# Differential and sparse attention: query tiles from token 16 in falling order, and one tile of 16 meta tokens

## The chip, the cores and the metric

The kernel runs on one core of one Trainium2 chip. The metric is the device time of one execution in microseconds (us), from the first to the last instruction of the program and what lies around them. Three runs of the kernel before gave 2288.31, 2290.07 and 2291.01 us; their median, 2290.07 us, is the time before.

## The reference, cut to what matters

The program is a stack of six layers on 512 tokens of 1024 channels: a Mamba-2 mixer and a sliding-window attention first; then 16 learned meta tokens are put in front, which makes 528 tokens, and a differential attention, a feed-forward layer, a sparse attention and a second feed-forward layer follow. The change touches the two attentions over 528 tokens.

```python
# differential attention: 8 heads, two maps of 64 channels each, values of 128
s = jnp.einsum('bqhcd,bkhcd->bhcqk', qb, k)
s = jnp.where(k_pos[None, :] <= q_pos[:, None], s, -jnp.inf)     # causal
p = jax.nn.softmax(s, axis=-1)
a = p[:, :, 0] - lam * p[:, :, 1]
o = einsum('bhqk,bkhe->bqhe', a, v)
# sparse attention: 16 heads; an indexer scores the keys of each query
score = jnp.where(causal & (k_pos < N_META)[None, :], BIG_SCORE, score)
score = jnp.where(causal, score, -jnp.inf)
top_val, top_idx = lax.top_k(score, topk)        # topk = 128
p = softmax over those keys;  o = p @ v
```

Each token attends to itself and to earlier ones. In the sparse attention a token keeps the 16 meta keys and the best others, 128 in all, so a meta token sees plain causal attention among 16 keys. The result is the last 512 tokens after a final norm.

## The kernel before, in words

All five engines run programs written by hand, with semaphores between them; the order of the instructions in the source is the order on each engine. Activations lie transposed, channels on partitions and 528 tokens along the row. Every projection is three products of split float32 numbers (`product`, line 301): a high part of the weights is made by ACT (`high`, L260), a low part by DVE or POOL (`low_on_vector`, L276, `low`, L268), in slots that the weight stream of SP refills.

`pairs` is one stage of attention, called twice: with `diff` (prefix `da`, 8 heads) and without (prefix `dsa`, 8 pairs of heads of 64 channels). A turn of its loop does head (or pair) `s` and, beside it, the projections of head `s + 1`. Per head:

- ACT evicts the projections (L2004). With `diff`, ACT also issues four DMAs for the queries and four for the keys that swap their channels by 32 (L2011); without it, PE turns them by a product (`rot`, L1854). DVE makes the rotary sum (L2149 to L2158). PE transposes the values (L1862), ACT stores them (L2023, L2024); in the sparse stage ACT copies ready values (L2016, L2017).
- Five tiles of queries follow, `TILES[n]`: 128 queries from token 0, 128, 256 and 384, and 16 from token 512. For a tile that starts at token c with nq queries, keys 0 to c + nq are used. Per tile: scores on PE for two maps (`scores`, L1883) into one buffer S of PSUM, banks 2 to 5; DVE adds the mask and takes the maximum (L2171, L2174); ACT takes the exponential and the sum (`exps`, L2030); DVE divides (L2188 to L2198); PE transposes the result in blocks of 128 keys (`trans`, L1899); ACT copies the blocks (`store_pt`, L2038, L2040); PE multiplies them with the values (`pv`, L1912); ACT stores the output (`store_o`, L2045). `MAPS` is the order of the maps. With `diff` the two maps are joined before the transposes; without it each is transposed.

S is single: scores of tile n + 1 wait until both reductions of tile n are done. What PE does between them is written in `step` of the tensor program: projection pieces (24 matmuls, or two half pieces of 12) stand between tile n's scores and its transposes, and again before its `pv`. Tile 3's `pv` and tile 4's transposes and `pv` fall in the next turn. In the sparse stage the output lies in bank 3, columns 128 to 384, where tile 4's scores, 512 to 528, have their last 16 columns in the same bank; so `pv` of tile 3 waits for tile 4's reductions, and tile 4's scores for tile 2's output.

The last turn (`step(NI, lin=False)`) has no projections beside it, except that of the values in the differential stage.

`index` makes the sparse mask. Queries are taken from token 16 on in four chunks of 128; DVE takes eight maxima at a time and writes 0 or -1e30 into `kept` (L2451). `TILES` begins at token 0, so POOL moves `kept` by 16 partitions into `mb` with seven DMAs (`move`, L2269, L2270), and DVE waits for them at the sparse stage's first tile 1. DVE fills `mb` before (L2404 to L2406).

## Time and profile before

| | before |
|---|---|
| median of three runs | 2290.07 us |
| span of the profiled execution | 2287.3 us |
| PE busy | 2134.9 us (93%) |
| DVE busy | 1460.5 us (64%) |
| ACT busy | 1016.0 us (44%) |
| POOL busy | 47.9 us |
| differential loop, first scores of head 0 to those of head 7 | 789.18 to 999.40 us |
| sparse loop, the same | 1628.18 to 1817.02 us |

The profile names one execution. Its own time outside the span is not listed: the median lies 2.8 us above the span. PE is busy almost throughout, mostly with projections (L301). The two stages that are changed take 244 us (789 to 1033) and 217 us (1628 to 1845), two tenths of the time. In a row of a timeline the first number is the start in us from the beginning of the span, the second the duration, then engine, line, operation, output and inputs, shape and count; a bracket tells how long the engine stood idle before it, and what ended that. Matmul durations overlap a little, so differences of starts give the cost of one in a row of many.

### The profile page before, as it was taken

Reading aid. Unit: us, or ns where it says so; the run is one execution under the profiler, and the core shown is the slowest. Engines: PE = TensorE matmul, PEld = TensorE weight load, DVE = VectorE, ACT = ScalarE, POOL = GpSimd, SP = SyncE. Lnnn points to the kernel's source line nnn. Section 1 sums busy time; section 2 is a strip of 40 time slices with the busy share of each in tenths; the row PEclk is TensorE's granted clock in tenths of the full one; section 3 lists DMA queues with packets and bytes.
Section 4 is the critical chain, followed back from the end, with each engine's and each line's share of the span. In section 5 each row is a group of like instructions: output and inputs, shape, how many; then the busy total and the mean of one; then the engine's idle time right before and its main releaser. Section 6 shows DMA issues by size and latency. Waiting matters only on the chain. (4 is left out here: it accounts for less than half of the span.)

```text
span 2287.3 us, 39714 instructions
## 1 busy us (share of the span) xinstructions
PE 2134.9 (93%) x14439; PEld 1862.1 (81%) x14439; DVE 1460.5 (64%) x3050; ACT 1016.0 (44%) x1891; POOL 47.9 (2%) x37
## 2 busy tenths in 40 slices
PE   5999998889998799989999999999899889999998
PEld 3777786667766688869999999987777689999886
DVE  6677876547775777765566653369566656666532
ACT  3555563435553455653444432324455534444322
POOL 1000000000000000000000000122100000000000
PEclk8999998899999899979999999989999889999999
DMA  5533321252212222212323333401111122333331
GB/s 126 135 106 101 101 78 51 80 114 57 46 38 65 61 70 74 74 29 80 93 86 91 92 103 90 102 20 41 51 43 39 35 74 84 92 92 92 110 89 50
DMA packets 357001, 174.63 MB, mean 76 GB/s; under 512 B 60735, under 2 KB 352424, under 8 KB 356904
## 3 DMA queue, kind: packets, MB, share of 16 engines
q1 hardware_dynamic: 353192, 168.19, 26.9%
q10 hardware_dynamic: 3072, 4.33, 0.7%
q0 software_dynamic: 640, 0.87, 0.3%
q8 instruction: 55, 0.90, 0.2%
q14 instruction: 42, 0.34, 0.1%
HBM read 166.58 MB, written 2.16 MB: 74 GB/s over the span
## 5 line engine op out<-in xcount | busy, mean ns | idle before, releaser
L301 PE MATMUL ps<-h_parts,parts 128*128 128x264 f32 (+3 forms) x8576 | 1309.8, 311 | 31.0 <-DVE h_parts L670 12.0
L301 PEld LDWEIGHTS ps<-h_parts,parts 128*128 128x128 f32 x8576 | 1174.7, 191 | 124.7 <-issue 38.0
L260 ACT ACTIVATE parts<-ring 128x1024 fp32r<-128x1024 f32 (+1 forms) x282 | 307.3, 1092 | 687.6 <-PE ps L301 457.8
L276 DVE TENSOR_TENSOR parts<-ring,parts 128x1024 fp32r<-128x1024 f32 (+1 forms) x266 | 337.1, 1270 | 172.7 <-ACT parts L260 171.6
L301 PE MATMUL ps<-wide_parts,parts 128*128 128x264 f32 (+3 forms) x1040 | 323.4, 325 | 0.0
L301 PE MATMUL ps<-up_hidden,parts 128*128 128x264 f32 (+1 forms) x1056 | 241.4, 322 | 1.8 <-PEq L2512 1.8
L301 PEld LDWEIGHTS ps<-wide_parts,parts 128*128 128x128 f32 x1040 | 193.0, 191 | 16.3
L301 PEld LDWEIGHTS ps<-up_hidden,parts 128*128 128x128 f32 x1056 | 175.1, 188 | 17.4 <-issue 2.1
L2495 DVE TENSOR_TENSOR up_u<-ps,norm_rstd 128x264 f32<-128x264 f32 (+2 forms) x176 | 74.9, 427 | 160.5 <-PE ps L301 153.1
L2811 DVE TENSOR_TENSOR res<-ps,res 128x264 f32<-128x264 f32 (+3 forms) x56 | 25.9, 467 | 98.0 <-PE ps L301 91.6
L301 PE MATMUL ps<-gated_high,parts 128*128 128x512 f32 x256 | 82.5, 402 | 2.5 <-DVE wide_parts L1230 2.0
L1883 PE MATMUL ps<-wide 64*128 64x256 f32 (+5 forms) x384 | 75.4, 484 | 7.7 <-DVE wide L2158 6.7
L1899 PEld LDWEIGHTS ps<-cst,wide 128*128 128x128 f32 (+2 forms) x360 | 36.1, 146 | 52.5 <-issue 28.5
L1042 DVE SCALAR_TENSOR_TENSOR ssm_conv<-wide,vec,ssm_conv 128x512 f32<-128x512 f32 x96 | 71.9, 751 | 8.6 <-ACT ssm_dts L772 1.9
L2505 DVE SCALAR_TENSOR_TENSOR up_hidden_plain<-up_u,vec,up_hidden_plain 128x528 f32<-128x528 f32 (+1 forms) x88 | 66.9, 760 | 10.4 <-DVE up_hidden_plain L2503 4.0
L268 POOL TENSOR_TENSOR parts<-ring,parts 128x1024 fp32r<-128x1024 f32 x16 | 38.3, 2397 | 1562.8 <-ACT parts L260 1562.8
L2482 ACT ACTIVATE up_hidden_plain<-up_u,vec 128x528 f32<-128x528 f32 (+1 forms) x88 | 71.0, 807 | 0.0
L1899 PE MATMUL ps<-cst,wide 128*128 128x128 f32 (+2 forms) x360 | 52.5, 271 | 17.6 <-DVE wide L2198 9.0
L2171 DVE CUSTOM_DVE_ANT_0 wide<-ps,mb 128x128 f32<-128x128 f32 (+4 forms) x80 | 42.1, 526 | 37.9 <-PE ps L1883 35.4
L2503 DVE SCALAR_TENSOR_TENSOR up_hidden_plain<-up_u,vec,up_hidden_plain 128x528 f32<-128x528 f32 (+1 forms) x88 | 66.3, 753 | 0.0
L2030 ACT ACTIVATE wide<-wide,dsa_nm 128x128 f32<-128x128 f32 (+4 forms) x80 | 47.1, 591 | 37.2 <-DVE dsa_nm L2174 37.2
L301 PEld LDWEIGHTS ps<-gated_high,parts 128*128 128x128 f32 x256 | 49.0, 191 | 15.9 <-issue 3.5
(321 smaller groups left out, 2331.8 us busy)
## 6 DMA issues: line engine op xcount, KB each, us to landing
ring<-in_ffn_w_up SPq DMA_DIRECT2D x88, 512.0 KB, 3.8
ring<-in_ssm_w_in SPq DMA_DIRECT2D x48, 512.0 KB, 4.1
ring<-in_ffn_w_down SPq DMA_DIRECT2D x32, 704.0 KB, 4.6
ring<-in_da_w_qkv SPq DMA_DIRECT2D x24, 512.0 KB, 4.1
ring<-in_dsa_w_in SPq DMA_DIRECT2D x24, 512.0 KB, 3.8
ring<-in_att_w_in SPq DMA_DIRECT2D x40, 256.0 KB, 3.7
ssm_prefix<-prefix_rows SPq DMA_DIRECT2D x32, 256.0 KB, 4.1
ring<-in_ssm_w_out SPq DMA_DIRECT2D x16, 512.0 KB, 4.2
```

Of the source, the lines that this page charges most:

```text
L260: self.nc.scalar.activation(self.part(st, u, 0), self.slot(x, st.kt), ACT.Copy).then_inc(self.w_high, 1)
L276: self.nc.vector.tensor_tensor(self.part(st, u, 1), self.slot(u % st.ring, st.kt), self.part(st, u, 0).bitcast(F32), ALU.subtract).then_in ...
L301: m = self.nc.tensor.matmul(out, w[:, n], b, start=start and f == j == 0, stop=stop and f == st.kt - 1 and j == 2)
L1042: ins = v.scalar_tensor_tensor(acc, u[:, q, j:j + SEQ], k.col(V_CW + 32 * j + tile), acc, ALU.mult, ALU.add)
L1883: m = nc.tensor.matmul(S[0:nq, x, lo:hi], rop[h, 0, c:N], rop[h, 1, lo:hi], start=True, stop=True)
L1899: m = nc.tensor.transpose(TP[0:w, x, b * nq:(b + 1) * nq], pn[0:nq, x, a:a + w], k.ident[0:nq, 0:nq])
L2030: nc.scalar.activation(p[0:nq, x, 0:c + nq], p[0:nq, x, 0:c + nq], ACT.Exp, bias=nm[0:nq, x:x + 1], scale=0.125, accum_out=den[0:nq, x:x + ...
L2171: v.tensor_tensor_reduce(p[0:nq, x, 0:N], S[0:nq, x, 0:N], mask(n), 1.0, -3e38, ALU.add, ALU.max, accum_out=mx[0:nq, x:x + 1]).then_inc(se ...
L2482: nc.scalar.activation(cc[:, x, begin:T2], u[:, x, begin:T2], ACT.Identity, scale=k.col(w0 + t), bias=k.col(w2 + 2 * FT + t)).then_inc(s_t ...
L2495: v.tensor_tensor(u[:, x, 2 + c:2 + c + w], ps[:, 2 + (2 * x + b) % 4, 0:w], k.rstd[:, c:c + w], ALU.mult).then_inc(s_free, 1)
L2503: v.scalar_tensor_tensor(acc, u[:, x, 1 + begin:1 + T2], k.col(w0 + 2 * FT + t), acc, ALU.mult, ALU.add).then_inc(s_mid, 1)
L2505: v.scalar_tensor_tensor(acc, u[:, x, 2 + begin:2 + T2], k.col(w2 + t), acc, ALU.mult, ALU.add).then_inc(s_conv, 1)
```

## The change

A second table of tiles, `QUERIES`, serves the queries: 128 from token 400, 272, 144 and 16, in this order, then 16 from token 0. Keys and values stay in blocks that start at multiples of 128 (`blocks`), so a tile of queries that starts at 16 + 128 m ends with a block of 16 keys. The mask of the indexer has the same four tiles and is written in place into `mb`, in the order of use; the moves on POOL, their semaphore and the buffer `kept` go. For the first chunk the causal mask is added on DVE, since a query with fewer than 112 keys behind the meta tokens would keep later ones too. The meta tile takes its mask from `maskb`. The last block of tile 0's transposes, 16 rows by 128 columns per map, goes to bank 5 (`TPL`), and its copy `ptl` is 128 wide. Tile 4's scores are 16 wide and stay clear of bank 3, so the wait for tile 2's output before them and the wait for their reductions before tile 3's `pv` go. ACT increments a semaphore once more per head (`passed`).

```diff
--- before.py
+++ after.py
@@ -43,6 +43,7 @@
 TILES = [(a, min(P, T2 - a)) for a in range(0, T2, P)]
+QUERIES = [(META + a, P) for a in range(SEQ - P, -1, -P)] + [(0, META)]
 LAMBDA_INIT = 0.2
@@ -169,7 +170,6 @@
         self.granted = self.sem("refills_granted")
-        self.mask_moved = self.sem("mask_moved")
         self.passed = self.sem("waits_passed")
@@ -1788,7 +1788,7 @@
         pt, mx, nm, den, rd = sb("pt", [P, maps, 512]), sb("mx", [P, 2]), sb("nm", [P, 2]), sb("den", [P, 2]), sb("rd", [P, 2])
-        ptl = sb("ptl", [META, maps, META])
+        ptl = sb("ptl", [META, maps, P])
         osq, lnv, rstd = (k.wide[:, j, :] for j in range(19, 22)) if diff else (None,) * 3
@@ -1806,13 +1806,18 @@
         def mask(n):
-            c, nq = TILES[n]
-            return sheet[0:nq, SEQ - c:SEQ + nq] if diff else mb[0:nq, n, 0:c + nq]
+            c, nq = QUERIES[n]
+            if diff:
+                return sheet[0:nq, SEQ - c:SEQ + nq]
+            return mb[:, n, 0:c + nq] if c else k.maskb[0:nq, P:P + nq]
         O = ps[:, 7, :] if diff else ps[:, 3, P:3 * P]
 
+        TPL = ps[0:META, 5, P:3 * P].rearrange("p (x j) -> p x j", x=2)
+
         def blocks(n):
 
-            return [(b, *TILES[b]) for b in range(n + 1)]
+            c, nq = QUERIES[n]
+            return [(b, b * P, min(P, c + nq - b * P)) for b in range((c + nq + P - 1) // P)]
 
@@ -1823,13 +1828,9 @@
                 if not diff:
-                    first, move = pool_first
-                    first(pool)
-                    for m in range(1, 4):
-                        move(pool, m)
+                    pool_first(pool)
                     for at in ((0, 0), (0, 1), (1, 0)):
                         k.low(pool, st, at)
-                    move(pool, 4)
 
@@ -1863,7 +1864,7 @@
                 def scores(s, n):
-                    c, nq = TILES[n]
+                    c, nq = QUERIES[n]
                     N = c + nq
@@ -1871,8 +1872,6 @@
                         pe.wait_ge(sem["masked"], 10 * s + 2 * n)
-                        if n == 4 and not diff:
-                            pe.wait_ge(sem["o"], 5 * s + 3)
                         if n == 4:
@@ -1884,7 +1883,7 @@
                 def trans(s, n):
-                    _, nq = TILES[n]
+                    _, nq = QUERIES[n]
                     if n == 0:
@@ -1896,20 +1895,19 @@
                         for b, a, w in blocks(n):
-                            m = nc.tensor.transpose(TP[0:w, x, b * nq:(b + 1) * nq], pn[0:nq, x, a:a + w], k.ident[0:nq, 0:nq])
+                            to = TP[0:w, x, b * P:b * P + nq] if b < 4 else TPL[:, x, :]
+                            m = nc.tensor.transpose(to, pn[0:nq, x, a:a + w], k.ident[0:nq, 0:nq])
                     m.then_inc(sem["t"], 1)
...
                 def pv(s, n):
-                    _, nq = TILES[n]
+                    _, nq = QUERIES[n]
                     pe.wait_ge(sem["pt"], 5 * s + n + 1)
                     wait(pe, sem["o"], 5 * s + n)
-                    if n == 3 and not diff:
-                        pe.wait_ge(sem["masked"], 10 * s + 10)
                     for b, a, w in blocks(n):
...
                             d = slice(0, P) if diff else slice(64 * x, 64 * x + 64)
-                            r = pt[0:w, x, b * nq:(b + 1) * nq] if b < 4 else ptl[:, x, :]
-                            m = nc.tensor.matmul(O[d, 0:nq], vt[0:w, b, d], r, start=b == 0, stop=b == n)
+                            r = pt[0:w, x, b * P:b * P + nq] if b < 4 else ptl[:, x, :]
+                            m = nc.tensor.matmul(O[d, 0:nq], vt[0:w, b, d], r, start=b == 0, stop=w < P)
                     m.then_inc(sem["pv"], 1)
@@ -2024,23 +2022,22 @@
                 def exps(s, n):
-                    c, nq = TILES[n]
+                    c, nq = QUERIES[n]
                     for j, x in enumerate(MAPS):
...
                 def store_pt(s, n):
-                    _, nq = TILES[n]
                     act.wait_ge(sem["t"], 5 * s + n + 1)
                     wait(act, sem["pv"], 5 * s + n)
-                    if n == 4:
-                        nc.scalar.activation(ptl[:], TP[0:META, 0:maps, 4 * META:5 * META], ACT.Copy)
-                    w = min(n + 1, 4) * nq
-                    nc.scalar.activation(pt[:, :, 0:w], TP[:, 0:maps, 0:w], ACT.Copy).then_inc(sem["pt"], 1)
+                    if n == 0:
+                        nc.scalar.activation(ptl[:], TPL[:, 0:maps, :], ACT.Copy)
+                    w, rows = (min(5 - n, 4) * P, P) if n < 4 else (META, META)
+                    nc.scalar.activation(pt[0:rows, :, 0:w], TP[0:rows, 0:maps, 0:w], ACT.Copy).then_inc(sem["pt"], 1)
 
                 def store_o(s, n):
-                    c, nq = TILES[n]
+                    c, nq = QUERIES[n]
                     act.wait_ge(sem["pv"], 5 * s + n + 1)
@@ -2068,6 +2065,7 @@
                     act.wait_ge(sem["o"], 5 * s + 5)
+                    act.sem_inc(k.passed, 1)
                     nc.scalar.activation(osq, head(s), ACT.Square).then_inc(sem["osq"], 1)
@@ -2159,13 +2157,11 @@
                         k.low_on_vector(dve, st, st.after(s, 1, st.depth))
-                    for n, (c, nq) in enumerate(TILES):
+                    for n, (c, nq) in enumerate(QUERIES):
                         N = c + nq
...
                         dve.sem_inc(k.passed, 1)
-                        if not diff and n == 1 and isinstance(s, int) and s == 0:
-                            dve.wait_ge(k.mask_moved, 16 * 7)
                         for j, x in enumerate(MAPS):
@@ -2235,12 +2231,11 @@
     wiT, wi = k.wide[:, 16, :], sb("wi", [P, 5, NH])
-    kept = sb("kept", [P, CHUNKS, SEQ], BF16)
     kn, lnv, rstd = (k.wide[:, j, :] for j in (12, 13, 14))
...
         "lin_done", "lin_free", "wi_product", "squares", "summed", "rstd", "kn", "rot", "rope", "scores", "relu", "acc", "m"))
-    s_kept, s_moved = k.sem("idx_kept"), k.mask_moved
+    s_kept = k.sem("idx_kept")
     s_rtok = k.sem("idx_rstd_by_token")
@@ -2260,14 +2255,6 @@
         k.low_all(pool, vst)
-
-    def move(pool, m):
-
-        pool.wait_ge(s_kept, m)
-        if m > 1:
-            w = min(P * m, SEQ) - META
-            pool.dma_start(mb[META:P, m - 1, META:META + w], kept[0:P - META, m - 1, 0:w]).then_inc(s_moved, 16)
-        pool.dma_start(mb[0:META, m, META:META + P * m], kept[P - META:P, m - 1, 0:P * m]).then_inc(s_moved, 16)
 
@@ -2401,9 +2388,7 @@
         pre.dve(dve)
-        do(v.memset(mb[:], NEG))
-        do(v.memset(mb[:, 1:5, 0:META], 0.0))
-        do(v.tensor_copy(mb[:, 0, 0:P], k.maskb[:, P:2 * P]))
+        do(v.memset(mb[:, :, 0:META], 0.0))
         pre.rstd_ready(dve)
@@ -2448,10 +2433,15 @@
                 do(v.match_replace(row, m8[:], row, -3e38))
-            v.tensor_scalar(kept[:, n - 1, 0:N], row, -2e38, NEG, ALU.is_gt, ALU.mult).then_inc(s_kept, 1)
+            own = mb[:, CHUNKS - n, META:META + N]
+            if n == 1:
+                do(v.tensor_scalar(own, row, -2e38, NEG, ALU.is_gt, ALU.mult))
+                v.tensor_tensor(own, own, k.maskb[:, P:2 * P], ALU.add).then_inc(s_kept, 1)
+            else:
+                v.tensor_scalar(own, row, -2e38, NEG, ALU.is_gt, ALU.mult).then_inc(s_kept, 1)
             dve.wait_ge(s_kept, n)
         steps.end()
-    return sync_program, (pool_program, move), pe_program, act_program, dve_program
+    return sync_program, pool_program, pe_program, act_program, dve_program
 
@@ -2845,7 +2835,7 @@
         with ExitStack() as own:
-            mb = k.sb("mb", [P, 5, T2], BF16, own)
+            mb = k.sb("mb", [P, CHUNKS, T2], BF16, own)
             vall = k.sb("values", [P, 8, 5, P], F32, own)
```

PE's program in the differential loop, from the first scores of a head on. L1883 (now L1882) are the scores, L1862 (L1863) the value transposes, L301 a projection, L1919 (L1917) the squares of the head before. Before:

```order
L1883 MATMUL ps<-wide 128x128 x2
L1858 REGISTER_ALU
L91 REGISTER_ALU
L1862 MATMUL ps<-cst,wide 128x128 x4
L1862 MATMUL ps<-cst,wide 16x128
L279 ISA
L91 ISA
L301 MATMUL ps<-h_parts,parts 128x264 x24
L1919 MATMUL ps<-wide,cst 128x264 x2
```

Now:

```order
L1882 MATMUL ps<-wide 128x512 x2
L1882 MATMUL ps<-wide 128x16 x2
L1859 REGISTER_ALU
L92 REGISTER_ALU
L1863 MATMUL ps<-cst,wide 128x128 x4
L1863 MATMUL ps<-cst,wide 16x128
L279 ISA
L92 ISA
L301 MATMUL ps<-h_parts,parts 128x264 x24
L1917 MATMUL ps<-wide,cst 128x264 x2
```

The head's widest scores stand first; everything around them keeps its place.

The end of the same loop, from tile 2's `pv` (L1912, now L1910) to tile 3's transposes (L1899). Before:

```order
L1912 MATMUL ps<-da_pt,da_v 128x128 x3
L1873 REGISTER_ALU
L1883 MATMUL ps<-wide 16x512 x2
L1883 MATMUL ps<-wide 16x16 x2
L1894 REGISTER_ALU
L1899 MATMUL ps<-cst,wide 128x128 x4
```

Now:

```order
L1910 MATMUL ps<-da_pt,da_v 128x128 x3
L1874 REGISTER_ALU
L1882 MATMUL ps<-wide 16x16 x2
L1893 REGISTER_ALU
L1899 MATMUL ps<-cst,wide 128x128
L1899 MATMUL ps<-cst,wide 16x128
```

Tile 4's scores shrink from 528 to 16 columns, and tile 3 has two blocks instead of four.

The sparse loop, from the first scores to the first transposes. Before:

```order
L1883 MATMUL ps<-wide 128x128 x2
L301 MATMUL ps<-h_parts,parts 128x264 x12
L1873 REGISTER_ALU
L1883 MATMUL ps<-wide 128x256 x2
L1894 REGISTER_ALU
L1899 MATMUL ps<-cst,wide 128x128 x2
```

Now:

```order
L1882 MATMUL ps<-wide 128x512 x2
L1882 MATMUL ps<-wide 128x16 x2
L301 MATMUL ps<-h_parts,parts 128x264 x12
L1874 REGISTER_ALU
L1882 MATMUL ps<-wide 128x400 x2
L1893 REGISTER_ALU
L1899 MATMUL ps<-cst,wide 128x128 x4
L1899 MATMUL ps<-cst,wide 16x128
L1899 MATMUL ps<-cst,wide 128x128 x4
L1899 MATMUL ps<-cst,wide 16x128
```

Between tile 0's and tile 1's scores stands half a projection, as before; the transposes are ten instead of two.

## Rows read from the trace of the kernel before

**Rows 1.** Windows, core 0: busy time and instructions of each engine, granted clock, DMA.

```profile
820.00:999.00 179.00, 172.73 (x1326) 150.78 (x1324) 129.95 (x387) 104.27 (x290) 0.00 (x0) 1.00 0.24 68
1655.00:1800.00 145.00, 138.79 (x1175) 110.86 (x1174) 99.48 (x326) 77.24 (x215) 0.00 (x0) 1.00 0.18 47
1006.00:1034.00 28.00, 17.92 (x64) 10.66 (x64) 17.80 (x51) 15.05 (x39) 0.00 (x0) 0.56 0.00 1
```

**Rows 2.** Timeline of PE, one turn: start, duration, line, shape, idle and releaser.

```profile
849.87 0.49 PE L1883 MATMUL ps<-wide 64*128 64x128 f32 x4
...
855.67 0.32 PE L1899 MATMUL ps<-cst,wide 128*128 128x128 f32 x1
...
863.67 1.13 PE L1883 MATMUL ps<-wide 64*128 64x512 f32 x4
...
868.26 0.83 PE L1912 MATMUL ps<-da_pt,da_v 128*128 128x128 f32 x6
...
870.02 0.66 PE L1899 MATMUL ps<-cst,wide 128*128 128x128 f32 x4
...
873.44 1.06 PE L1912 MATMUL ps<-da_pt,da_v 128*128 128x128 f32 x8
...
875.13 0.41 PE L1899 MATMUL ps<-cst,wide 16*128 16x16 f32 x5 [0.64 <-DVE wide L2198]
...
879.74 0.49 PE L1883 MATMUL ps<-wide 64*128 64x128 f32 x4
```

**Rows 3.** Timeline of ACT, its DMA queue and DVE, the same turn.

```profile
852.47 0.39 ACT L2030 ACTIVATE wide<-wide,da_nm 128x128 f32<-128x128 f32 x1
...
853.95 0.35 DVE L2198 SCALAR_TENSOR_TENSOR wide<-wide,da_rd 128x128 f32<-128x128 f32 x1
...
868.88 2.44 ACTq L2011 DMA_DIRECT2D da_turned<-wide  x4
...
871.62 0.59 ACT L2040 ACTIVATE da_pt<-ps 128x512 f32<-128x512 f32 x1
...
872.10 0.72 ACT L2030 ACTIVATE wide<-wide,da_nm 16x528 f32<-16x528 f32 x1
...
874.23 0.76 DVE L2198 SCALAR_TENSOR_TENSOR wide<-wide,da_rd 16x528 f32<-16x528 f32 x1
...
878.59 0.71 DVE L2158 TENSOR_TENSOR wide<-wide 128x528 f32<-128x528 f32 x1
```

**Rows 4.** Timeline of PE, one turn of the sparse loop.

```profile
1708.12 0.49 PE L1883 MATMUL ps<-wide 64*128 64x128 f32 x4 [0.16 <-DVE wide L2158]
...
1710.19 0.70 PE L1883 MATMUL ps<-wide 64*128 64x256 f32 x4
...
1711.33 0.44 PE L1899 MATMUL ps<-cst,wide 128*128 128x128 f32 x2 [0.44 <-DVE wide L2192]
...
1724.05 1.08 PE L1883 MATMUL ps<-wide 64*16 64x512 f32 x8
...
1734.94 0.49 PE L1883 MATMUL ps<-wide 64*128 64x128 f32 x4 [0.15 <-DVE wide L2158]
```

**Rows 5.** Timeline of DVE, tile 4 of the same sparse turn.

```profile
1725.37 0.70 DVE L2171 CUSTOM_DVE_ANT_0 wide<-ps,mb 16x528 f32<-16x528 f32 x1 [3.08 <-PE ps L1883]
...
1728.12 0.48 DVE L2192 TENSOR_SCALAR wide<-wide,dsa_rd 16x528 f32<-16x528 f32 x1
```

**Rows 6.** Timeline of PE, last heads: differential first, then sparse.

```profile
999.40 0.49 PE L1883 MATMUL ps<-wide 64*128 64x128 f32 x4
...
1028.62 2.10 PE L1919 MATMUL ps<-wide,cst 128*128 128x264 f32 x4 [1.04 <-ACT wide L2071]
...
1806.84 1.78 PE L1912 MATMUL ps<-dsa_pt,dsa_v 128*64 128x128 f32 x16 [1.89 <-DVE dsa_mx L2171]
...
1817.02 0.80 PE L1883 MATMUL ps<-wide 64*128 64x128 f32 x4 [1.61 <-DVE wide L2158]
```

**Rows 7.** Timeline of DVE, between index stage and sparse loop.

```profile
1615.97 0.71 DVE L2149 TENSOR_TENSOR wide<-wide,rcos 128x528 f32<-128x528 f32 x1 [5.96 <-ACT wide L2004]
```

## The prediction, made before the changed kernel was run

> **What bounds the kernel now.** I read the page first: TensorE (PE) is the busiest engine and ends the program, so its waits are the first suspects. Then the windows over the two attention loops [rows 1]: in the differential loop PE is busy 172.73 of 179 us, in the sparse loop 138.79 of 145 us, both at granted clock 1.00; when a stage has no projection left beside its last head, PE falls to 17.92 of 28 us and the clock to 0.56, the lower level of 1.2 GHz. Then the timeline of one turn on every engine, since a loop's period can be closed by a chain that PE's busy share hides.
>
> Differential turn: from one first score product to the next are 879.74 - 849.87 = 29.87 us [rows 2]. Only one wait shows there, 0.64 us before the last tile's transposes, ended by DVE's division (L2198). The rows of ACT and DVE show what lies behind it [rows 3]. ACT issues four DMAs (L2011), 2.44 us, in which nothing else starts on it; only then come the copy of the transposes (871.62), the exponentials of tile 4 (872.10), DVE's division (874.23) and its rotary chain for the next head, done 878.59 + 0.71 = 879.30. The next first scores start at 879.74: this chain is 0.3 us from setting the period already.
>
> Sparse turn: 1734.94 - 1708.12 = 26.82 us, with small waits, the largest shown 0.44 us before the first transposes [rows 4].
>
> **The change, part by part: widths.** Before, a head's five tiles are 128, 256, 384, 512 and 528 keys wide (the last with 16 queries); after, 528, 400, 272, 144 and 16. 1808 columns become 1360. The blocks of 128 keys or less stay 15, but their order turns from 1, 2, 3, 4, 5 to 5, 4, 3, 2, 1. Prices at full clock [rows 2]: scores 0.49 us for 128 columns and 1.13 for 512, so 0.0017 us a column; a block of pV 1.06 - 0.83 = 0.23; a block of transposes (0.66 - 0.32) / 3 = 0.11 per map. The 16 extra keys of the new first tile need small matmuls with a 128-column load; no row shows them. The bounds are nothing and the 0.49 us of the 128-column product; I take 0.25.
>
> **Differential loop.** I cut the turn where pV of tile 2 starts (868.26), since ACT's issue stall follows there. The part before it is 868.26 - 849.87 = 18.39 us. Its scores get 64 more columns and the small matmuls, +0.35; pV of tiles 0 and 1 has 9 blocks instead of 3, +1.38; transposes of tiles 0 to 2 have 12 instead of 6, +0.66; about 0.4 of small gaps around the 512-column products and the first transposes goes (as walked product by product). 20.3 us, give or take 0.2. Does a wait appear in it? The widest tile is now first: value copies (L2023, L2024) on ACT hold its exponentials back, now to 852.47 - 849.87 = 2.6 us after the scores began, with 0.9 us longer scores to 3.5. From the exponential to the division's end the 528-wide tile takes 874.23 + 0.76 - 872.10 = 2.89 us, so transposes can go at 6.6. PE is there at 855.67 - 849.87 = 5.8 now (the transposes of tile 0 stand behind the value transposes, a projection, the squares and tile 1's scores), and with the longer scores at 6.8. No wait, by 0.2 us.
>
> The part after it is 11.48 us now, of which 0.64 is the wait. PE alone would need 10.84 less 0.9 (scores of 16 instead of 528 columns), 0.2 (two transposed blocks less), 0.45 (two pV blocks less), and 1.25 (the last tile has one block instead of five): 8.0 us. But the chain is: ACT reaches the copy of the transposes 871.62 - 868.26 = 3.36 us after the cut, whatever the tile; that copy is 256 instead of 512 wide, some 0.26 instead of 0.48 to the next instruction; from the exponential to the division's end it takes 2.89 us at 528 columns and 853.95 + 0.35 - 852.47 = 1.83 at 128, so 1.53 at 16 on that line. The division ends at 5.15. Then DVE's cosine products and four more rotary instructions, which are not changed, 878.59 + 0.71 - 874.99 = 4.31, and 0.15 for the semaphore. Sum 9.6. 20.3 + 9.6 = 29.9 against 29.87: **nothing gained in a loop in which PE loses work and most of a 0.64 us wait**. What PE saves becomes a wait of 0.9 us before the first scores, with some 0.6 left before the last transposes. The cover that hides the saving is this chain; if it had slack, the turn would be 20.3 + 8.0 = 28.3. If the 16-wide tile costs what 128 columns do, the turn is 0.3 longer. Seven turns: 0, between -11 and +2.
>
> Here a rule of the Trainium skill speaks against the change. The page VectorE: DVE Perf Modes, section on the TRN2 errata, says that an SBUF-source instruction of VectorE or ScalarE pays a fixed latency whatever its width, and advises tiles of at least 512 elements. The trace agrees in kind: 0.35 us at 128 columns against 0.76 at 528 [rows 3]. By the page's table, 224 + 16 cycles at 1.2 GHz, the small exponential would be estimated at 0.20 us; the sum would move by under 1 us in all.
>
> **Differential, last head.** No projection stands beside it, and its path is a chain of round trips, 1028.62 - 999.40 = 29.2 us [rows 6]. It loses 448 columns, each worth 0.0033 us of scores at the low clock (twice 0.0017), 0.001 of reduction, 0.0017 for two exponentials (0.72 us at 528), 0.001 of division: 0.007, so -3.1 us at most. Widths are partly hidden by spread copies and low parts between; I take -3.0, since the very narrow last round trips have nothing beside them; bounds -5 and 0.
>
> **Sparse loop.** One S buffer serves all tiles: tile 1's scores wait for tile 0's reductions. Scores of 528 columns end at 1.45 us; the first reduction starts 0.24 later (as 1725.37 does after the product that ends at 1725.13), at 1.69; both are done 1.6 on, so scores of tile 1 start at 3.33, and PE with only half a projection between (1710.19 - 1708.12 = 2.07 now, less 0.42 for the first product: 1.65) is ready at 3.03: a wait of 0.3. From the first reduction to the last division is 1728.12 + 0.48 - 1725.37 = 3.23 [rows 5]; the transposes can go at 4.98, PE is ready at 4.20: a wait of 0.8. These two replace the 0.44 and a smaller one. From first scores to the last tile's scores (15.93 us now [rows 4]): +0.35 scores, pV 12 blocks instead of 6 +1.32, transposes 14 instead of 10 on two maps +0.84, waits +0.4: 18.8. From there to the next head (10.89 now): scores of 16 instead of 528 -0.86, pV of two blocks instead of four -0.44, transposes 2 instead of 10 -0.49, last pV 4 instructions instead of 20 -0.6: 8.5. Turn 27.3, +0.5, six times +3.0. If both new waits (1.1 together) were hidden, the six turns would come to -3.5; if both doubled, to +9.5.
>
> **Last turn and last head of the sparse stage** [rows 6]. The seventh turn has the longer front (+2.4), and behind it no projection: there PE waits 1.89 us for the reduction because pV's output shares a bank with the 512:528 columns. That wait goes, and the narrow tile's chain shortens: 12.1 us from the last scores' end to 1817.02 become 9.3. Together -0.4. The last head by the same walk -0.4, because its blocks, of two maps, cost as much as they did at 1.2 GHz; at most -3 by the columns.
>
> **Index stage.** Two memsets and a copy shrink to one memset, the seven moves leave POOL's DMA queue (and the projection splits queued behind them on it no longer wait), the mask is written in place, one 128-column addition is added. DVE has 5.96 us idle after that stage, waiting for ACT's evictions [rows 7]: 0. What would be late if that cover were gone is the first rotary product. The extra semaphore increment on ACT: 0.
>
> **Sum**: 0 - 3.0 + 3.0 - 0.4 - 0.4 = -0.8 us on a span of 2287.3 us, which lies 2.8 us under the median of the runs, 2290.07. Forecast 2289.3 us, no change: this kernel's measurement tells no less than 0.2%, 4.6 us.
>
> **Rivals.**
> 1. *Faster: PE bounds the differential loop.* For it: PE 172.73 of 179 us busy there. Against: the chain over ACT's issues and DVE's rotary products. Turn 28.3, or 28.9 with the wait before the last transposes left: -11 to -7 us, time 2278 to 2282. A sparse loop whose two new waits are hidden gives -6.5, alone 2283. Together 0.26.
> 2. *Slower: the differential tail does not shrink.* The part before the cut grows 1.9 us for certain; the part after it shrinks only if a 16-wide tile's exponential, reduction and division are really short. For it: fixed latency. Against: 0.35 against 0.76 us. If they stayed as at 528 columns, only the copy would be shorter and the turn 1.4 longer: +10 us, 2299. It decides from 0.8 us a turn. 0.12.
> 3. *Slower: the sparse waits are double*: +6.5 us, 2296. For it: reduction, exponential and division of the widest tile stand there with half a projection beside them. Against: no part of their chain is unmeasured [rows 5]. 0.07. A granted clock that falls in these gaps would end here too; the differential loop keeps 1.00 with its 0.64 us wait.
> The forecast: 0.55. Its own range is 2285 to 2294. The 80% range reaches to the faster rivals and the near end of the slower: 2280 to 2297. Faster 0.26, same 0.55, slower 0.19.
>
> **What would show it.** Differential turn 29.9 us, PE waiting about 0.9 us for DVE's rotary sum (L2156 now) before 512-column scores: if that wait is missing and the turn is under 29, rival 1. Turn over 30.7: rival 2. Sparse turn 27.3 with waits of 0.3 (before scores of 400) and 0.8 (before the first transposes). No 1.89 us wait before the last pV products. Both last heads end earlier by 3.0 and 0.4. Most likely to be wrong: the 0.2 us margin at the first transposes, and the cold last heads, walked from hot prices.

## The result, and the profile after

| | before | changed |
|---|---|---|
| median of 20 runs each | 2288.89 us | 2293.10 us |
| ratio of the two, 95% interval | | 1.0021 [1.0012, 1.003] |
| span of the profiled execution | 2287.3 us | 2292.6 us |
| PE busy | 2134.9 us | 2138.0 us |
| DVE busy | 1460.5 us | 1440.5 us |
| differential stage, first scores to first output product (da_out) | 244.90 us | 246.84 us |
| sparse stage, the same (dsa_out) | 217.05 us | 221.23 us |
| differential turn, in the loop | 29.85 us | 30.39 us |
| sparse turn, in the loop | 26.82 us | 27.66 us |

By the ratio the changed kernel is 0.21% slower, about 4.8 us of 2289 (the two medians differ by 4.2), and the interval lies clear of 1. Forecast was no change, 2289.3 us. The median of after lies inside the range that was given, but there is a loss where none was forecast: the terms that had to cancel did not.

Windows after: the first two over the same stretches as [rows 1], the third inside the last differential head, where no projection stands (columns as there: PE, PEld, DVE, ACT, POOL busy, granted clock, DMA share, GB/s):

```profile
820.00:999.00 179.00, 173.36 (x1317) 152.77 (x1317) 117.69 (x383) 101.34 (x289) 0.00 (x0) 1.00 0.25 68
1655.00:1800.00 145.00, 136.31 (x1130) 109.37 (x1129) 91.23 (x306) 72.45 (x200) 0.00 (x0) 1.00 0.16 44
1014.00:1030.00 16.00, 11.09 (x42) 6.97 (x42) 10.32 (x40) 8.70 (x27) 0.00 (x0) 0.50 0.00 1
```

Over these stretches DVE has 12 us less work in the differential loop and 8 less in the sparse loop, as the narrower tiles promise; it bought nothing. Windows over exactly one turn tell more. First one differential and one sparse turn of before, then the same of after:

```profile
879.74:909.59 29.85, 28.90 (x223) 25.24 (x222) 22.18 (x65) 17.91 (x50) 0.00 (x0) 1.00 0.25 71
1708.12:1734.94 26.82, 25.59 (x219) 20.50 (x219) 18.22 (x58) 14.27 (x39) 0.00 (x0) 1.00 0.15 39
```

```profile
882.06:912.46 30.40, 29.21 (x223) 25.77 (x223) 20.73 (x65) 17.50 (x51) 0.00 (x0) 1.00 0.24 70
1710.98:1738.64 27.66, 26.13 (x218) 21.06 (x218) 17.08 (x58) 14.13 (x39) 0.00 (x0) 1.00 0.14 38
```

The columns of scores of a head fell by a quarter (1808 to 1360), and PE's busy time rose: by 0.3 us a differential turn and by 0.54 a sparse one. The rest of each turn's growth (0.24 and 0.30) is waiting.

The end of a differential turn after, which answers to [rows 2, 3]: timelines of PE, of ACT with its queue, and of DVE (start, duration, line, idle time ahead and what ended it).

```profile
872.16 1.02 PE L1910 MATMUL ps<-da_pt,da_v 128*128 128x128 f32 x6
...
876.43 0.80 PE L1910 MATMUL ps<-da_pt,da_v 128*128 128x128 f32 x4
877.44 0.17 PE L1899 MATMUL ps<-cst,wide 16*16 16x16 f32 x1 [0.21 <-DVE wide L2194]
...
882.06 0.70 PE L1882 MATMUL ps<-wide 64*128 64x512 f32 x2 [0.98 <-DVE wide L2156]
```

```profile
872.78 2.44 ACTq L2009 DMA_DIRECT2D da_turned<-wide  x4
875.35 0.28 ACT L2042 ACTIVATE wide<-ps 128x128 f32 x1 [1.66 <-issue]
875.53 0.38 ACT L2037 ACTIVATE da_pt<-ps 128x256 f32<-128x256 f32 x1
875.79 0.29 ACT L2028 ACTIVATE wide<-wide,da_nm 16x16 f32<-16x16 f32 x1
```

```profile
877.07 0.22 DVE L2194 SCALAR_TENSOR_TENSOR wide<-wide,da_rd 16x16 f32<-16x16 f32 x1
877.61 1.33 DVE L2147 TENSOR_TENSOR wide<-wide,da_rcos 128x528 f32<-128x528 f32 x2 [0.31 <-issue]
...
881.30 0.71 DVE L2156 TENSOR_TENSOR wide<-wide 128x528 f32<-128x528 f32 x1
```

Read upward from the last row of each: the scores wait 0.98 us for DVE's rotary sum (881.30 + 0.71). That rotary chain starts behind tile 4's division. The division waits for an exponential, and the exponential stands behind 2.44 us of DMA issue. One link is no work at all: for 0.31 us DVE stands between two instructions with no releaser but "issue".

The sparse turn after, PE alone, which answers to [rows 4]:

```profile
1710.98 1.26 PE L1882 MATMUL ps<-wide 64*128 64x512 f32 x8 [0.15 <-DVE wide L2156]
...
1714.06 0.94 PE L1882 MATMUL ps<-wide 64*128 64x400 f32 x4 [0.17 <-DVE dsa_mx L2167]
1715.84 1.31 PE L1899 MATMUL ps<-cst,wide 128*128 128x128 f32 x10 [0.84 <-DVE wide L2188]
...
1718.55 1.09 PE L1910 MATMUL ps<-dsa_pt,dsa_v 128*64 128x128 f32 x16
1719.57 0.43 PE L1910 MATMUL ps<-dsa_ptl,dsa_v 16*64 16x128 f32 x4
...
1723.07 1.24 PE L1910 MATMUL ps<-dsa_pt,dsa_v 128*64 128x128 f32 x16
...
1726.95 1.02 PE L1910 MATMUL ps<-dsa_pt,dsa_v 128*64 128x128 f32 x12
...
1733.26 0.80 PE L1910 MATMUL ps<-dsa_pt,dsa_v 128*64 128x128 f32 x8
```

Against them the rows of pV before, in the turn of [rows 4], for tiles of one, two, three and four full blocks:

```profile
1713.20 0.44 PE L1912 MATMUL ps<-dsa_pt,dsa_v 128*64 128x128 f32 x4
...
1716.46 0.66 PE L1912 MATMUL ps<-dsa_pt,dsa_v 128*64 128x128 f32 x8
...
1720.71 0.88 PE L1912 MATMUL ps<-dsa_pt,dsa_v 128*64 128x128 f32 x12
...
1728.17 1.09 PE L1912 MATMUL ps<-dsa_pt,dsa_v 128*64 128x128 f32 x16
```

The two waits are those that were forecast. The pV rows hold what was not: four full blocks take 1.09 us, and three full blocks with one of 16 keys behind them take 1.24; so 1.02 against 0.88 and 0.80 against 0.66.

The stage times also hold a disturbance that comes in some executions only. In the first differential turn after (788.94 to 821.64, 32.70 us against 30.16 before), four DMAs took 3.70 us to issue instead of 2.44; PE waited 0.61 and 0.51 us, and then the granted clock fell for four microseconds. Windows of after:

```profile
816.00:818.00 2.00, 1.49 (x9) 1.41 (x9) 1.93 (x5) 0.45 (x2) 0.00 (x0) 0.74 0.41 129
818.00:820.00 2.00, 2.00 (x11) 2.00 (x11) 1.90 (x4) 0.00 (x0) 0.00 (x0) 0.50 0.00 0
820.00:822.00 2.00, 2.00 (x14) 1.77 (x15) 0.61 (x1) 0.57 (x2) 0.00 (x0) 0.90 0.00 0
```

A projection of 24 products that takes 3.18 us elsewhere took 4.71 there. Four more profiled executions below have the same code in this turn. In e1 and e7 the issue took 2.45 us, no such wait came, and the turn took 30.47 and 30.52. In e9 and e11 the issue took 3.96 and 3.76 us, the waits and the fall of the clock came again, and the turn took 32.97 and 32.85. The two executions with the old code of this stage that issue from ACT (before, e2) had 30.16 and 30.19. What lengthens the issue is not known, nor is it shown that the old code never meets it. A stage's total of one execution carries some 2.4 us of this; the turns inside the loops repeat to 0.03 us, and the experiments are read by them.

### The profile page after: what moved, and what is told of

It reads as the page before. It is cut to its first block and busy times, and to the rows that moved or that the text cites. A ratio compares the mean times of both kernels' runs of the same rounds, so it can differ in the third digit from the quotient of the medians.

```text
span 2292.6 us, 39704 instructions
## 1 busy us (share of the span) xinstructions
PE 2138.0 (93%) x14439; PEld 1867.5 (81%) x14439; DVE 1440.5 (63%) x3049; ACT 1012.3 (44%) x1891; POOL 44.6 (2%) x30
## 3 DMA queue, kind: packets, MB, share of 16 engines
q1 hardware_dynamic: 353192, 168.19, 26.8%
## 5 line engine op out<-in xcount | busy, mean ns | idle before, releaser
L301 PE MATMUL ps<-h_parts,parts 128*128 128x264 f32 (+3 forms) x8576 | 1310.2, 311 | 31.0 <-DVE h_parts L670 11.9
L301 PEld LDWEIGHTS ps<-h_parts,parts 128*128 128x128 f32 x8576 | 1174.9, 191 | 126.1 <-issue 38.8
L276 DVE TENSOR_TENSOR parts<-ring,parts 128x1024 fp32r<-128x1024 f32 (+1 forms) x266 | 337.1, 1270 | 172.0 <-ACT parts L260 170.9
L301 PE MATMUL ps<-wide_parts,parts 128*128 128x264 f32 (+3 forms) x1040 | 324.1, 326 | 0.0
L301 PE MATMUL ps<-up_hidden,parts 128*128 128x264 f32 (+1 forms) x1056 | 241.4, 322 | 1.7 <-ACTq L2502 0.9
L301 PEld LDWEIGHTS ps<-wide_parts,parts 128*128 128x128 f32 x1040 | 193.6, 192 | 16.3
L301 PEld LDWEIGHTS ps<-up_hidden,parts 128*128 128x128 f32 x1056 | 175.1, 188 | 17.4 <-issue 2.1
L301 PE MATMUL ps<-gated_high,parts 128*128 128x512 f32 x256 | 82.4, 402 | 2.6 <-DVE wide_parts L1230 2.0
L1882 PE MATMUL ps<-wide 64*128 64x16 f32 (+5 forms) x384 | 62.6, 416 | 14.3 <-DVE wide L2156 11.4
L1899 PE MATMUL ps<-cst,wide 128*128 128x128 f32 x360 | 57.3, 290 | 11.8 <-DVE wide L2188 7.3
L1899 PEld LDWEIGHTS ps<-cst,wide 128*128 128x128 f32 x360 | 36.0, 130 | 35.6 <-issue 18.0
L2167 DVE CUSTOM_DVE_ANT_0 wide<-ps,da_causal 128x528 f32<-128x528 f32 (+4 forms) x80 | 34.7, 434 | 44.7 <-PE ps L1882 44.1
L301 PEld LDWEIGHTS ps<-gated_high,parts 128*128 128x128 f32 x256 | 49.0, 191 | 16.0 <-issue 3.5
L2002 ACT ACTIVATE wide<-ps 128x264 f32<-128x264 f32 x80 | 30.7, 385 | 67.2 <-PE ps L301 65.2
```

The costliest lines, as they stand in the source:

```text
L276: self.nc.vector.tensor_tensor(self.part(st, u, 1), self.slot(u % st.ring, st.kt), self.part(st, u, 0).bitcast(F32), ALU.subtract).then_in ...
L301: m = self.nc.tensor.matmul(out, w[:, n], b, start=start and f == j == 0, stop=stop and f == st.kt - 1 and j == 2)
L1882: m = nc.tensor.matmul(S[0:nq, x, lo:hi], rop[h, 0, c:N], rop[h, 1, lo:hi], start=True, stop=True)
L1899: m = nc.tensor.transpose(to, pn[0:nq, x, a:a + w], k.ident[0:nq, 0:nq])
L2167: v.tensor_tensor_reduce(p[0:nq, x, 0:N], S[0:nq, x, 0:N], mask(n), 1.0, -3e38, ALU.add, ALU.max, accum_out=mx[0:nq, x:x + 1]).then_inc(se ...
```

## Experiments

Theory A, formed on these traces: a differential turn is closed by a chain through ACT, DVE and PE, not by PE's work; the differential tail holds ACT's DMA issue in it, and the sparse turn pays for PE's work on 16-key blocks and for waits behind the widest tile. Rivals: the loss sits in one stage only, or in other stages; PE's own work closes the loops; or order alone is the cause. All medians are set against runs of before on the same chip.

### One stage at a time (e1, e2)

```diff
-            pairs(k, "da", S["da"], following["da"], True, update, spread=heads)
+            pairs_da(k, "da", S["da"], following["da"], True, update, spread=heads)
...
# e1: the kernel before, pairs_da being pairs of the changed one
# e2: the changed kernel, pairs_da being pairs of the kernel before
```

> The differential stage alone takes the new query tiles; the index and the sparse stage stay as before. Theory A (each stage loses on its own: the loops are closed by a chain over ScalarE, VectorE and the first scores, not by TensorE): this kernel is about 1.7 us slower than before (first da_out product +1.7 us: turns 210.2 to 214.3 us, last head -2.1), the wait of TensorE ahead of the first scores 0.98 us in a steady turn of 30.39. Rival B (the whole loss is in the sparse stage, and the differential shift is the clock of that one execution): within 0.5 us of before. Rival C (the tables in SBUF and the longer program cost the other stages too): more than 3 us slower.

> The index and the sparse stage alone take the new tiles; the differential stage stays as before. Theory A: +4.2 us in the sparse stage (first sparse scores to first dsa_out product 217.05 to 221.2 us; steady turn 26.8 to 27.66), whole time 3 to 4 us over before. Rival B: all of it, +4.8 us. Rival C (only the first turns and the ends differ, and steady turns are the same within 0.2 us when on the same chip): under 1.5 us slower.

Measured: e1 1.0004 [0.9993, 1.0015], median 2288.33; e2 1.0019 [1.001, 1.0028], median 2291.97. Turns in e1: differential 30.39, sparse 26.8; in e2: 29.87 and 27.66. So a stage's turn does not care what the other stage does. **The loss that the whole time shows is the sparse stage's**, 4.3 us (2.3 to 6.4). The differential stage is worth +0.9 us, -1.6 to +3.4: not told from nothing. In the traces its turns cost more (first scores of head 0 to head 7: 212.13 us in e1, 210.22 before, 210.00 in e2), and its last head gives it back (30.82 us to the first da_out product, 34.68 before and in e2). Its first turn in e1 was one of the undisturbed ones. Rival B, which put all of it in the sparse stage, is as good a reading of the times as A.

### The DMA issue out of the chain (e3, e4)

```diff
             def _(pool):
+                if diff:
+                    for i in range(NI):
+                        for u in range(2):
+                            pool.wait_ge(sem["lin_free"], NP * i + 2 * u + 2)
+                            wait(pool, sem["rope"], 2 * i - 1 + u if i else 0)
+                            for r in range(0, P, 32):
+                                pool.dma_start(turned[r ^ 32:(r ^ 32) + 32, u, :], raw[r:r + 32, u, :]).then_inc(s_turned[u], 16)
...
-                                if diff and j < 4:
-                                    turn(i, j // 2)
```

> The changed kernel with the eight DMAs a head that fill the turned copy of the query and key tiles in the differential stage issued by the idle GpSimd engine, and not by ScalarE (nothing is left out). Theory A (the differential turn is closed by ScalarE's 2.44 us of DMA issue, then the last tile's copy, exp and division, then the rotary chain): the last tile's exp starts about 2.4 us earlier, the 0.98 us wait ahead of the first scores goes, and TensorE bounds the turn at 28.9 to 29.4 us: 6 to 9 us faster than the changed kernel. Rival D (TensorE's own work and its other waits close the loop): the turn stays at 30.4 within 0.3 us. Rival E (GpSimd's issue is slow, so that the turned copy of the key arrives late): the turn is longer, the second rotary product waits for the DMA, 2 us or more slower.

> The kernel before with the same DMAs issued by GpSimd in the differential stage (nothing is left out). Theory A: before, the issue lay beside TensorE's work, whose wait ahead of the first scores was short, so a turn gains at most 0.6 us: 2 to 5 us faster than before over seven turns, clearly less than the same edit gives the changed kernel. Rival D: the turn stays at 29.85 within 0.3 us. Rival E: slower by 2 us or more, as in the changed kernel.

Measured: e3 0.9985 [0.9977, 0.9994], against 1.0021 without the edit; e4 0.9988 [0.9979, 0.9997]. Turns: e3 29.45 in the loop, from 30.39, and 29.0 to 29.1 outside it, but for the first, 31.12, which began at a granted clock of 0.50 that held some 6.5 us; e4 29.63, from 29.85. One turn of e3, then two rows of its DMA issue on GpSimd:

```profile
879.83:909.28 29.45, 29.04 (x222) 25.72 (x222) 20.64 (x65) 17.34 (x50) 3.93 (x8) 1.00 0.26 72
```

```profile
861.34 1.96 POOL L1836 DMA_DIRECT2D da_turned<-wide  x4 [16.71 <-ACT wide L2009]
871.74 1.96 POOL L1836 DMA_DIRECT2D da_turned<-wide  x4 [8.44 <-ACT wide L2009]
```

PE's 29.04 us of work is now nearly the whole turn, but 0.41 us of waiting for DVE's rotary sum are left, so that the turn lies just over the 28.9 to 29.4 expected. The exponential starts 1.86 us after tile 2's pV instead of 3.63 (in e3 from 870.86), and the division ends at 4.20 instead of 5.13: 2.44 us of issue bought 0.93. DVE's split of the weights (L276, 1.23 us, 872.84 to 874.07) now stands where the exponential stood, and the reciprocal for the division starts behind it, at 873.98. Theory A held: the same edit is worth 0.94 us a turn to the changed kernel and 0.22 to the kernel before. In e3 rivals D and E fell. In e4 E fell, but 0.22 lies within the 0.3 that D allowed, and only the whole time (2.7 us, 0.7 to 4.8) speaks against D there.

### The same engine, another place (e10)

```diff
+                            if diff and lin and q == 5:
+                                turn(i, 1)      # behind exps(s, 4), no longer in pieces()
```

> The changed kernel with ScalarE still issuing the DMAs of the turned tiles in the differential stage, but those of the key tiles (four in each head from the second) behind the last tile's exp and not ahead of its copy; nothing is left out. Theory A (it is the place of the 2.44 us issue in the closing chain that costs, not which engine does it): the last tile's exp starts about 2.4 us earlier, and the turn falls from 30.39 to 29.3 to 29.7 as long as the turned key tile still lands before VectorE's second rotary product. Rival F (the DMA lands too late now): VectorE waits for it, the wait ahead of the first scores grows over 0.98, turn 30.4 to 31.5. Rival D (the issue was never in the chain): turn unchanged at 30.39.

Measured: turn 30.24 us, whole time 1.0018 [1.0007, 1.0029]. The exponential starts 1.85 us after tile 2's pV (897.96) instead of 3.63, 1.8 us earlier and not 2.4, and the division ends 0.93 earlier, as in e3. But DVE's chain now stops for the DMA; its timeline in e10:

```profile
902.47 1.33 DVE L2149 TENSOR_TENSOR wide<-wide,da_rcos 128x528 f32<-128x528 f32 x2 [0.31 <-issue]
903.94 0.71 DVE L2154 TENSOR_TENSOR wide<-da_turned,da_rsin 128x528 f32<-128x528 f32 x1
904.68 0.71 DVE L2158 TENSOR_TENSOR wide<-wide 128x528 f32<-128x528 f32 x1
906.21 0.71 DVE L2154 TENSOR_TENSOR wide<-da_turned,da_rsin 128x528 f32<-128x528 f32 x1 [0.81 <-DMA da_turned<-wide]
```

Less that 0.81 us the turn would be 29.43, which is e3's 29.45. My 29.3 to 29.7 missed because of this landing: 906.21 lies 3.7 us after the last issue ended (902.52). That is rival F's mechanism: PE's wait ahead of the first scores grew from 0.98 to 1.19 us, though the turn stayed below F's 30.4. The chain is confirmed, and moving its stall inside ScalarE only trades it.

### DVE's loop written out (e7)

```diff
-                with dve.Fori(2, NI - 2) as s:
-                    step(s)
+                for s in range(2, NI - 2):      # the differential stage alone
+                    step(s)
```

> The changed kernel with VectorE's four looped turns of the differential stage written out one after another (nothing is left out). Theory: the 0.31 us that VectorE idles for its loop's branch, between the last division and the cosine products, stands in the closing chain now, so that the differential turn goes from 30.39 to 29.95 us in the turns that were looped, and the wait ahead of the first scores from 0.98 to 0.55; 1.2 to 1.8 us in all, too little for the whole time to tell. Rival: the gap is hidden, as it was before, and the turn stays at 30.39.

Measured: the three turns of 30.39 take 29.90; the wait ahead of the scores is 0.49. Whole time 1.001 [0.9998, 1.0021], not told apart from either kernel. The cosine products begin right behind the division (875.59, the division from 875.44 on for 0.22 us), and from the division's end to the end of the rotary sum pass 4.22 us instead of 4.72. So the gap of 0.31 us and what goes with it at the end of DVE's loop stood in the chain. Before, at the same place, the cosine products began at 874.91, right behind the 528-wide division of [rows 3]: there the gap did not show.

### Start and order apart (e5, e6)

```diff
-QUERIES = [(META + a, P) for a in range(SEQ - P, -1, -P)] + [(0, META)]
+QUERIES = [(META + a, P) for a in range(0, SEQ, P)] + [(0, META)]            # e5
...
+ORDER = [3, 2, 1, 0, 4]                         # e6: before, TILES[ORDER[n]] for TILES[n]
```

> The changed kernel with its query tiles still beginning at token 16, but in rising order (144, 272, 400, 528 keys, then the meta tile), in both stages; nothing is left out. The sparse stage needs two waits moved with it, since the 528-key scores now come beside an output. Theory W (in the sparse turn of 27.66 us the loss of 0.84 is 0.54 of TensorE's own work for the four 16-key blocks, which stays, and 0.30 of waits, which the falling order adds): sparse turn 27.2 to 27.4, the waits of 0.84 and 0.17 us replaced by short ones ahead of the first transposes. Rival O (the order is all of it): sparse turn 26.8. In the differential stage the theory of the closing chain says that the front is short again and the tail is that of a 16-key tile: the turn becomes 29.0 to 29.6, bound by TensorE; a rival says that the tail closes the loop whatever stands ahead of it: 30.4.

> The kernel before with its query tiles still beginning at token 0 but the four tiles of 128 in falling order (512, 384, 256, 128 keys), then the 16 queries with 528 keys as before; nothing is left out. Theory W: no 16-key blocks, so TensorE's work is that of before (25.6 us in the sparse turn), and the falling order costs its 0.3 us of waits: sparse turn 27.0 to 27.2. Rival O (the order is all of it): 27.6. Rival P (the blocks are all of it): 26.8. Differential stage: the front is long and the tail is the long one of 528 keys: the turn becomes longer than either kernel's, 31.0 to 32.0 us.

Measured: e5 1.0032 [1.002, 1.0045]; e6 1.0059 [1.0047, 1.0072]. The sparse turn falls apart into work and waits:

| sparse turn, us | turn | PE busy | the rest |
|---|---|---|---|
| start 0, rising (before) | 26.82 | 25.59 | 1.23 |
| start 16, falling (changed) | 27.66 | 26.13 | 1.53 |
| start 16, rising (e5) | 27.67 | 26.15 | 1.52 |
| start 0, falling (e6) | 27.39 | 25.69 | 1.70 |

The work follows the start, 0.44 to 0.56 us by pair, whatever the order: that half of theory W is shown. My numbers for the turns were 0.3 too low in both, because the waits are not a property of the order alone. In e5 the 528-key scores have to wait for an output in the same bank, which cost 0.56 us ahead of them; in e6 the falling order costs 0.47 and not 0.3. Rivals O and P fell: neither order nor blocks are all of it.

In the differential stage e6 gave two values. Three turns took 30.35, where 31 to 32 was expected: PE's idle went to one wait of 1.64 us ahead of the last transposes, and the chain behind it ran beside the last projection. Three others took 32.50 (the first), 31.83 and 31.90, and this is not the chain but the granted clock. Two turns of e6 from that wait on:

```profile
939.84 0.41 PE L1900 MATMUL ps<-cst,wide 16*128 16x16 f32 x5 [1.64 <-DVE wide L2201]
940.18 3.18 PE L302 MATMUL ps<-h_parts,parts 128*128 128x264 f32 x24
...
970.19 0.41 PE L1900 MATMUL ps<-cst,wide 16*128 16x16 f32 x5 [1.64 <-DVE wide L2201]
970.53 4.73 PE L302 MATMUL ps<-h_parts,parts 128*128 128x264 f32 x24
```

The wait is the same, and so is the work ahead of it; the clock stayed at 1.00 in the first and fell to 0.50 for some 3.5 us in the second, which made the projection 1.55 us longer. All seven turns of e6 have this wait (1.58 to 1.64), and it was followed by the fall in three. So two turns fell into the expected range, but for a reason that was not given. e5 missed: it gave 30.41 and not 29.0 to 29.6. Its waits in one turn (line waited for, us, times, longest):

```profile
PE ps L1863 <- ACT wide L2046: 0.6, 1, 0.6
PE ps L1901 <- DVE wide L2198: 0.3, 1, 0.3
```

The first is the value transposes standing for the last head's output copy. With the scores no longer late, the next wait in the ring appears at once, and at full clock all four orders lie at 29.85 to 30.43 in the loop.

### The short blocks left out (e9)

```diff
-            return [(b, b * P, min(P, c + nq - b * P)) for b in range((c + nq + P - 1) // P)]
+            return [... if diff or not c or b * P < c + nq - META]   # sparse: no last 16 keys
```

> The changed kernel, but in the sparse stage the four tiles of 128 queries leave out the last 16 keys of each: neither their transposes nor their products with the values are made (part of the computation is left out, and the output differs). Theory: a block of 16 keys costs TensorE what a full one does, 0.22 us of transposes and 0.36 to 0.43 us of products, four times a turn: TensorE's busy time in the sparse turn falls from 26.13 to about 23.7 us and the turn from 27.66 to 25.4 to 25.9, about 13 us over the stage. Rival 1 (the blocks are small and cheap): busy time falls by under 1 us. Rival 2 (VectorE and ScalarE close the sparse turn): busy time falls but waits take its place, and the turn stays over 27.0.

Measured, with the values of 16 keys missing in every such tile: sparse turn 25.58 us, PE busy 23.94, whole time 0.9933 [0.9916, 0.9949]. One turn of e9:

```profile
1708.49:1734.08 25.59, 23.94 (x195) 19.60 (x195) 17.04 (x58) 14.10 (x39) 0.00 (x0) 1.00 0.15 41
```

Work fell by 2.19 us and the turn by 2.08, so in the sparse turn PE's work counts nearly one for one, and sixteen keys cost 2.19 / 4 = 0.55 us a tile. Both rivals fell.

### The projection beside the widest tile (e11)

```diff
-        slots = [parts[0:2]] + [parts[j:j + 1] for j in range(2, 8)]
+        slots = [parts[0:1], parts[1:2], parts[2:4]] + [parts[j:j + 1] for j in range(4, 8)]
```

> The changed kernel with one half projection of the sparse stage moved: two half projections stand between the scores of the widest tile and those of the next, and one instead of two beside the meta tile (nothing is left out). Theory: the waits of 0.17 us before the 400-column scores and 0.84 before the first transposes come from having only half a projection beside the widest tile's reduction, exponential and division; with 1.65 us more work there both go. Beside the meta tile the division ends 0.1 us after TensorE could use it, and the rotary chain ends about 1.6 us earlier, so that 0.1 to 0.3 us of wait comes back: sparse turn 26.8 to 27.0 instead of 27.66, 4 to 5 us in all. Rival (what goes at the front comes back at the tail, because VectorE's chain closes the turn): 27.5 to 27.7.

Measured: 0.9974 [0.9963, 0.9985], sparse turn 26.77 us. Timeline of PE in e11, front and end of a turn:

```profile
1710.67 3.18 PE L301 MATMUL ps<-h_parts,parts 128*128 128x264 f32 x24
1713.78 0.94 PE L1882 MATMUL ps<-wide 64*128 64x400 f32 x4
1714.66 1.31 PE L1899 MATMUL ps<-cst,wide 128*128 128x128 f32 x10
...
1733.48 1.16 PE L1855 MATMUL ps<-wide,cst 128*128 128x264 f32 x4 [0.37 <-ACT wide L2042]
```

Both waits at the front are gone and nothing of them came back at the tail. The turn is 0.89 shorter at the same work (26.15 busy). Six such turns are 5.3 us, and the sparse stages of the two traces differ by 4.9 (221.23 and 216.37). The whole time fell by more: from 1.0021 to 0.9974, with 6.2 us between the near ends of the intervals. The two ratios come from different chips, and the profiled execution of e11 was the longest of its eight (2290.40 against a median of 2284.62), so its stages are not those of the median. What lies beyond the turns is left open.

### Put together (e8, e12)

e8 is e1 with the edits of e3 and e7 (new tiles in the differential stage alone); e12 is the changed kernel with those of e3, e7 and e11.

> A version meant to beat both: the new tiles in the differential stage alone, its DMAs for the turned tiles issued by the idle GpSimd engine, VectorE's loop of that stage written out, and the index and sparse stages of before. Theory A: every differential turn 29.0 us (TensorE's work, no wait), first scores to the first da_out product about 237.5 us against 244.9 before, the sparse stage as before at 217 us: 2280 to 2284 us, 5 to 8 us faster than before, and 2 to 4 faster than the kernel before with the same DMAs moved. Rival: without the order's cost in the sparse stage nothing else changes and the first head and the last give back what the turns gain: 2286.

> The changed kernel, new tiles in both stages, with three things moved: the turned tiles' DMAs on GpSimd, VectorE's differential loop written out, and the half projection of the sparse stage beside the widest tile (nothing is left out). Theory: differential turn 29.0 us, sparse turn 26.8 to 27.0: 2276 to 2279 us, the same within 0.1% as the version with the sparse stage of before (2276.8). Rival: sparse turn 27.66 still, 2281 to 2283.

Measured: e8 0.9955 [0.9938, 0.9971], median 2276.84; e12 0.9954 [0.9938, 0.9969], median 2277.73. Both beat both kernels. Windows over one differential turn and one sparse turn of e12:

```profile
878.50:907.54 29.04, 29.04 (x224) 25.73 (x223) 20.39 (x65) 17.35 (x50) 3.93 (x8) 1.00 0.26 73
1698.03:1724.80 26.77, 26.14 (x219) 21.11 (x219) 17.09 (x58) 14.35 (x39) 0.00 (x0) 1.00 0.14 39
```

The differential turn has no wait left: PE busy 29.04 of 29.04. There the new order is 0.6 us a turn better than the old one with the same DMAs moved (e4, 29.63; its turn outside DVE's loop took 29.62, so that the branch has no part in this). But little of it is work saved on PE. Without its wait of 0.38 us ahead of the last transposes, e4's turn would be 29.25, as the kernel before without its 0.64 would be 29.23. So the new order saves PE some 0.2 us a turn from start to start, and nothing by its busy time (28.99 in e4); the rest is a wait that is gone. The median of e8 is 3 us under the near end of what was expected; its stages were 235.00 and 213.96 us, 2.5 and 3 shorter than I had them. For the sparse stage, whose code is that of before, this is again the place at which the clock fell: its seventh turn took 25.81 us, with the clock at 1.00 to its end.

## Why the prediction was wrong

**The differential turn.** Forecast 29.9, measured 30.39. The closing chain was right part for part, from one cut to the next: front 20.49 (20.3), ACT at the copy 3.37 after the cut (3.36), division ended 5.13 after it (5.15), PE waiting 0.98 us for DVE's sum (0.9), 0.21 left before the last transposes (0.6). The 0.2 us margin at the first transposes, named as most likely to be wrong, held. What was missing in the chain is 0.41 between the division's end and the end of the rotary sum: 882.01 - 877.29 = 4.72 instead of 4.31. In e7, without the loop, the same stretch is 4.22. I took the rotary rows of before as a fixed price, though they stood behind a wide instruction that hid the gap. Term "seven turns: 0": +1.9 in e1, +4.1 in the profiled execution with its disturbed first turn.

The other side of this term failed too, though the chain hid it: "PE alone" was reckoned at 20.3 + 8.0 = 28.3 us, 0.9 below the 29.23 of before. e8, in which nothing but PE bounds the turn, shows 20.53 + 8.49 = 29.02. Of the 0.5 us missing behind the cut, 0.19 is pV of the 272-key tile, whose block of 16 keys was priced as a full one, 0.14 stands in the starts of the two projections, and most of the rest in the last tile. There was next to no gain for the chain to hide.

**The differential last head.** Forecast -3.0; -2.1 in after, -3.9 in e1. Right, as far as the clock lets it be read: the two differ in when the granted clock fell (0.89 in the first 11 us of it after, 1.00 in e1), and before it was at 0.60 there.

**The sparse turn: the step that failed.** Forecast 27.3, measured 27.66, +5.6 us over six turns instead of +3.0. The waits were right: 0.17 and 0.84 for 0.3 and 0.8, and +0.30 in all for the +0.4 that I summed. Wrong was "pV 12 blocks instead of 6 +1.32 ... pV of two blocks instead of four -0.44". I priced every block at the 0.22 us of a full one. The four 128-query tiles take 1.45 (its two rows overlap by 0.07) + 1.24 + 1.02 + 0.80 = 4.51 us of pV, and took 0.44 + 0.66 + 0.88 + 1.09 = 3.07: +1.44 where I had +0.88. Each of the four blocks of 16 keys costs 0.36 us, 0.14 more than a full one. These 0.56 us, less 0.14 of scores and 0.1 of waits that were cheaper than I had them, are the missing 0.36 within 0.04. For the small matmuls in the scores I had given bounds, for those in pV none: the one form that no row showed was taken for a known one.

**Seventh turn and last sparse head.** Forecast -0.4 and -0.4, read as -2.11 and +0.67. Of the first, most is not the edit: the code of before took 28.64 us in its own trace, with the clock at 0.50 from the 1.89 us wait on, and 25.78 in e1, where the clock fell some 6 us later; the changed code took 25.73 in e2. By these two the edit is worth nothing there. The old code also took 28.63 (e4) and 25.81 (e8), the changed code 26.51 to 26.70 in e3, e7 and e10, so that the term stays open within the clock's 2.9 us. The last head (28.21 before, 28.88 after, 26.55 in e2) moves more with the clock than with the edit; its term stays open.

**Index stage.** Forecast 0. From the first da_out product to the first sparse scores: 594.10 us before and 592.29 after, but 596.27 in e1 with the old code and 594.30 in e2 with the new. Over all traces it lies between 593.69 and 598.40 with the old code and between 592.27 and 598.44 with the new. No effect is told from this spread.

**Rivals.** Rival 1 was wrong as it stood. Its 28.9 us turn is near the 29.03 of e8 and e12, but by luck: it was 28.3 of work and 0.6 of a wait, and they have 29.03 of work and no wait. Rival 2 was called from a turn of 30.7; the tail did shrink. Rival 3's waits did not double, and so the slower side came by a way that I had not listed, two small terms of 0.4 us a turn. Forecasting no change from +3.0 and -3.0, the first of which came out 2.6 too low, left the slower side too little at 0.19.

## What to carry to other kernels

A loop that is closed by a chain gives nothing for work removed beside the chain: find the link that has no arithmetic in it (here 2.44 us of DMA issue on ScalarE) and move it first, and expect the next link to take over (it bought 0.94 us a turn). Then count the work of the busiest engine in instructions and not in columns: here a quarter of the columns went and TensorE's busy time did not fall. When a tile boundary shifts, the ragged block is paid in every tile and not once; price it by its own row or leave it a bound. When the widest tile moves to the front of a pipeline, move the filler work there with it.
